# The branch outputs of a hybrid block, parted: pool branch in straight products, delta branch in seven products of halves

## The chip, the cores and the metric

One core of one Trainium2 chip. The metric is the device time of one execution, in microseconds. The engines work side by side, each in order: TensorE (PE) multiplies, VectorE (DVE) and ScalarE (ACT) work on tiles, GpSimd (POOL) and SyncE (SP) mostly start DMAs.

## The reference, cut to what matters

One layer over 16 meta tokens and 512 tokens of width 2048, all float32:

```python
proj = xn @ w_in                       # splits: pool, delta net, gate_pool, gate_dn
y_pool = pooling_mixer(...) * silu(z_pool)        # width 1024
y_dn = gated_deltanet_branch(...)                 # width 2048
merged = sigmoid(gate_pool) * (y_pool @ w_pool_out) + sigmoid(gate_dn) * (y_dn @ w_dn_out)
h = h + merged @ w_o
out = rmsnorm(h[:, N_META:], final_norm_w)
```

The change concerns the line of `merged`: two products, 1024 and 2048 deep, both 2048 wide, over 512 tokens.

## The kernel before, in words

Float32 products at the rate of the short formats: each operand is split into a high part (`xh`, `wh`: a rounded copy, made by ScalarE, line 1198) and a low part (`xl`, `wl`: the difference, made by VectorE, L1753), and each product of tiles is three matmuls: high by high, low by high, high by low. The weight tile (128 x 128) is stationary; the tokens are the moving columns.

**The projection stage** runs 56 blocks of 256 output columns (`NCP`). Most blocks use seven products of halves (the Strassen-Winograd scheme): weights in four quarters, tokens in two halves, contraction in two halves; sums of weight quarters (S1 to S4: `s1`..`s4`, VectorE, L1761 to L1783), sums of x halves made once at the start, seven products numbered 7, 6, 2, 5, 4, 3 and 1 (`NEXT`: product 1 of the following block, issued at the end of the present one), and sums of results (C11, C21, C22). Each product is two chunks of 12 matmuls over 256 tokens (264 where meta tokens count); a ring of five slots (`RINGS`) holds split weights, filled about four chunks ahead (`AHEAD`). The 14 x sets (seven high, seven low) lie in SBUF through the stage (`XPLACE`). The last 16 blocks are the gates: ScalarE puts each through a sigmoid and stores it to `gates_scratch` in DRAM (`gate_tail`, L1583). The two branches' outputs are in DRAM as well (`branch_scratch`, 3072 rows).

**The branch outputs** (`window_b`) replace the x sets by 24 row tiles of `yraw`, split into `yh` and `yl` inside the last gate block and the first windows. Eight pairs of output column tiles `jp`, two tiles `c` each, and three units `u` of 8 row tiles (`u` = 0: pool branch, 1 and 2: delta branch). SP loads each unit's 1 MB of weights, ScalarE and VectorE split it, PE runs 24 matmuls of 512 columns per unit, into bank 0 of `pj[c]` for the pool branch and bank 1 for the delta branch. `merge` on VectorE multiplies both banks with their gates (loaded by POOL's queue, `gate_load`) and adds them into `merged`, which is split into `mh`, `ml` on the way.

**The last product** (`tile_terms`) multiplies `merged` with `w_o`: 4 blocks of 512 columns, 16 row tiles, 4 token tiles, 3 terms; residual, norm and output follow.

Everything on an engine is in the written order; engines meet by semaphores. `pe_chunk` counts chunks, `lo_done` split weights, `peb` finished units.

## Time and profile before

| what | us |
|---|---|
| median of 3 runs | 1894.07 (1891.62 to 1894.8) |
| the profiled execution | 1893.61 |
| its span, first to last instruction | 1891.9 |
| PE busy | 1839.9 (97%) |
| DVE busy | 1294.1 (68%) |
| ACT busy | 996.4 (53%) |
| POOL busy | 120.0 (6%) |

Rows of a profile name a line of the kernel, an engine, an operation and the tiles, output first (`out<-in`). Matmuls are pipelined, so each lasts longer than the distance to the next; a group's mean duration is not what one costs. The granted clock is 1.00 at 2.4 GHz and 0.50 at 1.2 GHz.

### The profile page before, as it was taken

The page shows a single profiled execution, that of the slowest core. Times are in us where ns is not written, and L with a number is a line of the kernel's source. Part 1 is how long each engine was busy: PE and PEld are TensorE (multiplying, and loading weights), DVE is VectorE, ACT ScalarE, POOL GpSimd, SP SyncE. Part 2 cuts the span into 40 slices and gives each one's busy share as a digit, 9 for nine tenths or more (in the row PEclk, how much of TensorE's full clock was granted, in tenths as well). Part 3 has the DMA queues.
Part 4 walks back from the last instruction along what each step waited for, and adds up shares of the span by engine and source line. Part 5 has one row for each costly group of instructions (what it writes and reads, how often), then busy time and mean ns, then how long its engine had stood idle before and what let it go on. Part 6 is the DMA issues. An engine that isn't in the chain of part 4 may idle for free.

```text
span 1891.9 us, 38102 instructions
## 1 busy us (share of the span) xinstructions
PE 1839.9 (97%) x15313; PEld 1727.3 (91%) x15313; DVE 1294.1 (68%) x2404; ACT 996.4 (53%) x2303; POOL 120.0 (6%) x156
## 2 busy tenths in 40 slices
PE   6999999999999999999999999999999999999998
PEld 6999999999899999999999998999998888888886
DVE  7777878777787887878788786777778444344342
ACT  6445456566575756757566675654546222223231
POOL 1100000101010010101001010000000000000000
PEclk9999999999999999999999999999999999999999
DMA  6342465555274555537545454467455434347202
GB/s 190 102 134 64 115 164 149 133 149 155 88 196 137 158 134 145 159 91 197 147 145 136 136 142 133 123 180 201 127 146 165 146 124 142 118 137 289 89 23 89
DMA packets 311000, 264.92 MB, mean 140 GB/s; under 512 B 12201, under 2 KB 266626, under 8 KB 310178
## 3 DMA queue, kind: packets, MB, share of 16 engines
q1 hardware_dynamic: 283712, 197.24, 36.4%
q0 software_dynamic: 12992, 39.57, 7.6%
q10 hardware_dynamic: 14130, 25.81, 3.8%
q8 instruction: 115, 1.88, 0.4%
q14 instruction: 51, 0.42, 0.1%
HBM read 221.03 MB, written 42.60 MB: 139 GB/s over the span
## 4 chain that ended last, share of the span: by engine, by line
PE 76%; DVE 10%; ACT 6%; issue 4%; DMA 3%; POOL 0%; ACTq 0%; DVEq 0%; SPq 0%; POOLq 0%
PE pj L873 35%; PE pj L800 18%; PE pj L832 10%; PE pg L800 10%; PE pt L800 3%; DVE wl L1753 2%; ACT wh L1198 2%; DVE raw L1783 1%; DMA raw<-in_w_in 1%; PE pt L1005 1%; DVE stg L2097 1%; DMA st<-gram_scratch 1%; ACT ktok L1436 1%; ACT L1453 1%; DVE f L1887 0%
## 5 line engine op out<-in xcount | busy, mean ns | idle before, releaser
L873 PE MATMUL pj<-xh,wh 128*128 128x256 f32 (+2 forms) x2568 | 747.7, 291 | 6.7 <-ACT snap L1198 3.0
L873 PE MATMUL pj<-xl,wh 128*128 128x256 f32 (+2 forms) x2568 | 723.5, 282 | 0.0
L873 PE MATMUL pj<-xh,wl 128*128 128x256 f32 (+2 forms) x2568 | 723.4, 282 | 0.0
L1753 DVE TENSOR_TENSOR wl<-raw,wh 128x512 fp32r<-128x512 f32 x742 | 501.0, 688 | 280.7 <-ACT wh L1198 273.1
L1198 ACT ACTIVATE wh<-raw 128x512 fp32r<-128x512 f32 x742 | 452.1, 626 | 401.6 <-PE pj L873 163.9
L873 PEld LDWEIGHTS pj<-xh,wh 128*128 128x128 f32 x2568 | 483.9, 188 | 15.1 <-ACT snap L1198 5.3
L873 PEld LDWEIGHTS pj<-xl,wh 128*128 128x128 f32 x2568 | 484.7, 189 | 0.7 <-issue 0.7
L873 PEld LDWEIGHTS pj<-xh,wl 128*128 128x128 f32 x2568 | 483.5, 188 | 0.0
L832 PE MATMUL pj<-xh,wh 128*128 128x260 f32 (+2 forms) x648 | 186.3, 287 | 3.1 <-DVE wl L1753 3.1
L832 PE MATMUL pj<-xh,wl 128*128 128x260 f32 (+2 forms) x648 | 184.1, 284 | 0.0
L832 PE MATMUL pj<-xl,wh 128*128 128x260 f32 (+2 forms) x648 | 183.8, 284 | 0.0
L1198 ACT ACTIVATE bwh<-rawb 128x256 fp32r<-128x256 f32 x192 | 64.9, 405 | 170.4 <-PE pj L800 169.9
L800 PE MATMUL pj<-yh,bwh 128*128 128x512 f32 x384 | 150.5, 392 | 3.4 <-DVE yl L2301 2.4
L800 PE MATMUL pj<-yl,bwh 128*128 128x512 f32 x384 | 150.0, 391 | 0.0
L800 PE MATMUL pj<-yh,bwl 128*128 128x512 f32 x384 | 149.9, 390 | 0.0
L2296 DVE TENSOR_TENSOR bwl<-rawb,bwh 128x256 fp32r<-128x256 f32 x192 | 69.0, 419 | 85.4 <-ACT bwh L1198 85.4
L832 PEld LDWEIGHTS pj<-xh,wh 128*128 128x128 f32 x648 | 123.2, 190 | 3.6 <-POOL xl L2430 3.4
L832 PEld LDWEIGHTS pj<-xl,wh 128*128 128x128 f32 x648 | 123.4, 191 | 0.2 <-issue 0.2
L832 PEld LDWEIGHTS pj<-xh,wl 128*128 128x128 f32 x648 | 123.0, 190 | 0.0
L2097 DVE SCALAR_TENSOR_TENSOR stg<-xin,convcur,stg 128x528 f32<-128x528 f32 x144 | 109.8, 762 | 8.5 <-ACT stg L1402 7.7
L800 PEld LDWEIGHTS pj<-yh,bwh 128*128 128x128 f32 x384 | 72.5, 189 | 19.3 <-DVE yl L2301 3.3
L800 PEld LDWEIGHTS pj<-yh,bwl 128*128 128x128 f32 x384 | 72.5, 189 | 15.3
(304 smaller groups left out, 2409.3 us busy)
## 6 DMA issues: line engine op xcount, KB each, us to landing
raw<-in_w_in SPq DMA_DIRECT2D x224, 512.0 KB, 4.6
head_scratch<-stg ACTq DMA_DIRECT2D x64, 264.0 KB, 4.1
rawb<-in_w_dn_out SPq DMA_DIRECT2D x16, 1024.0 KB, 6.0
rawb<-in_w_o SPq DMA_DIRECT2D x12, 1024.0 KB, 5.1
kq<-head_scratch SPq DMA_DIRECT2D x8, 1056.0 KB, 9.8
gates_scratch<-stg ACTq DMA_DIRECT2D x32, 256.0 KB, 2.0
rawb<-in_w_pool_out SPq DMA_DIRECT2D x8, 1024.0 KB, 5.3
yraw<-branch_scratch SPq DMA_DIRECT2D x6, 1024.0 KB, 7.7
```

What stands on the lines that cost most here:

```text
L800: return pe.matmul(dst, lhs, rhs, start=start, stop=stop)
L832: mm = pe.matmul(banks[bank][:, c0:TH], w[:, slot, k, :], xx[factor][:, kt, c0:TH], start=chunk in opened and one and k == 0, stop=chunk i ...
L873: mm = pe.matmul(bank[:, c0:TH], w[:, slot, k, :], xx[what][:, kt, c0:TH], start=opens and one and kt == 0, stop=closes and last and kt == ...
L1005: mm = pe.transpose(pt[rows, i * P:(i + 1) * P], src, ident)
L1198: return act.activation(dst, src, ACT.Copy)
L1436: act.activation(ktok[:, at, :], src, ACT.Copy, scale=cur[:, EDEC, at:at + 1]).then_inc(tok_done, 1)
L1453: act.activation(dec[:, 0:XC], dec[:, 0:XC], ACT.Exp, scale=-1.0)
L1753: tt(wl[:, slot, :, :], raw[:, buffer_of(of, par, what), HK * half:HK * (half + 1), :], wh[:, slot, :, :].bitcast(F32), ALU.subtract).then ...
L1783: tt(tile, tile, raw[:, buffer_of(b, par, 2), :, :], ALU.add).then_inc(sum_done, 1)
L2097: dve.scalar_tensor_tensor(acc, xin[:, src_tap:src_tap + T], w, acc, ALU.mult, ALU.add).then_inc(conv_step, 1)
L2296: tt(bwls[u][:, 2 * q:2 * q + 2, :], rawbs[u][:, 2 * q:2 * q + 2, c * P:(c + 1) * P], bwh[:, u, 2 * q:2 * q + 2, :].bitcast(F32), ALU.subt ...
```

## The change

The branch outputs are parted.

*Units.* 16 units of one output column tile each compute `y_pool @ w_pool_out` straight (8 row tiles, 24 matmuls of 512 columns), in turn into the banks `pg[0..2]` and `pt`. VectorE multiplies each with its gate (`unit_weighed`, in place in one of three gate buffers), POOL stores it to `pool_out_scratch` in DRAM, waits for that and loads the gate three units on. Meanwhile VectorE and ScalarE build the seven x sets of the delta branch's output from two buffers `yd`, four steps per unit (`set_steps`, four sums and seven splits for each of four quarters).

*Delta blocks.* `y_dn @ w_dn_out` runs as 8 more blocks of the projection's code (`DN0` to `END`), after a block `PRE` that holds only the first product 1. Their results land in `merged`; VectorE multiplies them with their gates in place (`weighed_by_gate`), and POOL adds the stored pool tiles by an accumulating DMA. The splits of `merged` move: four inside the delta blocks, twelve beside the last product's first block. In the last product the tiles of `w_o` and the splits have other places; the residual rows and the norm's row are loaded ahead of the fifth part of `w_o` and not after the sixth.

The last gate block loses its `yl` parts; eight pool row tiles are split in the gate blocks 10 to 13 (`y_part`), two per block. The loops of `window_b` over column pairs are gone, the new work is written out.

```diff
+ORDER_ALONE = (NEXT,)
...
+PRE = NCP
+DN0 = PRE + 1
+END = DN0 + D // CW
...
+    if b == PRE:
+        return ORDER_ALONE
+    return ORDER_LAST if b in (NCP - 1, END - 1) else ORDER
...
+        NUNIT = D // P
+        SET_SUMS = ((7, "f12", "f22"), (6, "x7", "f11"), (5, "f12", "f11"), (4, "x6", "f21"))
+        SET_SPLITS = (1, 2, 3, 7, 6, 5, 4)
+        STAGE = len(SET_SUMS) + len(SET_SPLITS)
...
+        def unit_buffer(n):
+
+            return 2 if n < 2 else n // 2 % 2
+
+        def unit_ring(n):
+
+
+            return (2, 0)[n % 2]
+
+        def unit_gate(n):
+
+            return (n + 2) % 3
...
+        def m_ready(k):
+
+
+            return mg_done[k // 2 % 2], 32 * (k // 4 + 1)
...
+            def load_unit(jp):
+
+                buffer = unit_buffer(2 * jp)
+                sp.dma_start(unit_raw[buffer], w_pool_out[0, :, jp * CW:(jp + 1) * CW].rearrange("(k p) c -> p k c", p=P)
+                             ).then_inc(w_loaded[buffer], 16)
...
+            sp.wait_ge(lo_done, ALL_SPLITS)
+            load_unit(1)
+            load_unit(2)
+            sp.wait_ge(w_lo, 4)
+            load_stage(0)
             for c in range(2):
                 sp.wait_ge(gate_stored[c], 16 * NGATE)
-            sp.dma_start(yraw[:, 20:24, :], y_rows[:, 20:24, :]).then_inc(yraw_tail, 16)
-            for jp in range(1, D // CW):
-                load_b(jp, False)
+            load_stage(1)
+            sp.wait_ge(w_lo, 8)
+            load_unit(3)
+            sp.wait_ge(x_lo, SET_LO + 3)
+            load_stage(2)
+            sp.wait_ge(w_lo, 12)
+            load_unit(4)
+            sp.wait_ge(x_lo, SET_LO + len(SET_SPLITS) + 3)
+            load_stage(3)
+            for jp in range(5, NUNIT // 2):
+                sp.wait_ge(w_lo, 4 * jp - 4)
+                load_unit(jp)
+            for units, pieces in ((NUNIT - 2, ((RA, 11), (buffer_of(DN0, DN0 % 2, 7), 21))),
+                                  (NUNIT, ((RF, 22), (buffer_of(DN0, DN0 % 2, 2), 12)))):
+                sp.wait_ge(w_lo, 2 * units)
+                for slot, quarter in pieces:
+                    load_raw(slot, quarter, 0, w_dn_out)
+            for b in range(DN0, END - 1):
+                block_loads(b, b % 2, (b + 1 - DN0) * CW, None, w_dn_out)
...
+            pe.wait_ge(y_ready, 2 * PAIRS)
+            pe.wait_ge(x_lo, Y_LO + UK)
+            unit_banks = [pg[0], pg[1], pg[2], pt]
+            for n in range(NUNIT):
+                need(pe, unit_done, n - 3)
+                for half in range(2):
+                    pe.wait_ge(w_lo, 2 * n + half + 1)
+                    for k in range(HK):
+                        kt, ring = HK * half + k, unit_ring(n) + half
+                        for w, yy, one, last in ((wh, yh, True, False), (wh, yl, False, False), (wl, yh, False, True)):
+                            mm = product(unit_banks[n % 4][:, :], w[:, ring, k, :], yy[:, kt, :], one and kt == 0, last and kt == UK - 1)
+                mm.then_inc(w_used, 1)
+
+            for b in range(PRE, END):
+                block_products(b, b % 2, "gate", "gate", no_hook)
...
+                        if b == DN0:
+                            act.wait_ge(unit_stored, 16 * NUNIT - 16)
+                        act.wait_ge(add_done, added(b - 3 if b == DN0 + 1 else b - 2, "C11"))
                         copy(snap[:, par, c0:TH], bank_a[par][:, c0:TH]).then_inc(snap_done, 1)
...
+                        if b == DN0:
+                            act.wait_ge(unit_stored, 16 * NUNIT)
+                        need(act, add_done, added(previous(b), "C22"))
                         copy(snap[:, 3, c0:TH], bank_b[:, c0:TH]).then_inc(snap_done, 1)
...
+            for n in range(NUNIT):
+                if n < NUNIT - 1:
+                    for half in range(2):
+                        unit_split(n + 1, half)
+                else:
+                    for at in range(2):
+                        split_hi(PRE, 0, at)
+                for q, step in set_steps(n):
+                    if step >= len(SET_SUMS):
+                        set_split(q, step - len(SET_SUMS))
+            for at in range(3):
+                split_hi(DN0, DN0 % 2, at)
...
+            def m_split(k):
+
+                act.wait_ge(*m_ready(k))
+                if 4 <= k < 12:
+                    act.wait_ge(pe_chunk, base_of(END))
+                copy(mhs[k], merged[:, k, :]).then_inc(m_hi, 1)
+
+            for b in range(DN0, END):
+                def branch(t, b=b):
+                    j = b - DN0
+                    if t == 0 and j > 0:
+                        last_to_time(b - 1, 1 - b % 2, "gate", merged[:, 2 * j - 2, :])
+                    if t in (4, 6) and j in (4, 5):
+                        m_split(2 * (j - 4) + t // 2 - 2)
+                    if b == END - 1 and t in C_SPLITS:
+                        split_c(0, C_SPLITS.index(t))
+                block_acts(b, b % 2, "gate", "gate", branch, no_hook)
+            last_to_time(END - 1, (END - 1) % 2, "gate", merged[:, KT - 2, :])
...
+            def unit_low(n, half):
+
+                dve.wait_ge(w_hi, 2 * n + half + 1)
+                slot = unit_ring(n) + half
+                own = unit_raw[unit_buffer(n)][:, HK * half:HK * (half + 1), P * (n % 2):P * (n % 2 + 1)]
+                tt(wl[:, slot, :, :], own, wh[:, slot, :, :].bitcast(F32), ALU.subtract).then_inc(w_lo, 1)
+
+            def unit_weighed(n):
+
+                dve.wait_ge(g0_loaded[unit_gate(n)], 16 * (n // 3) + 16)
+                dve.wait_ge(w_used, n + 1)
+                gate = g0[unit_gate(n)]
+                tt(gate, gate, (pg[0], pg[1], pg[2], pt)[n % 4][:, :], ALU.mult).then_inc(unit_done, 1)
+
...
+            gate_block(NCP - 1, 1, into_units, no_hook)
+            dve.wait_ge(pe_chunk, ALL_CHUNKS)
+            for n in range(NUNIT):
+                if n < NUNIT - 1:
+                    for half in range(2):
+                        unit_low(n + 1, half)
+                else:
+                    for at in range(2):
+                        split_lo(PRE, 0, at)
+                if n > 0:
+                    unit_weighed(n - 1)
+                if n == NUNIT - 1:
+                    s3(DN0, DN0 % 2)
+                for q, step in set_steps(n):
+                    set_step(q, step)
+            for at in range(2):
+                split_lo(DN0, DN0 % 2, at)
+            unit_weighed(NUNIT - 1)
+            s2(DN0, DN0 % 2)
+            split_lo(DN0, DN0 % 2, 2)
+
...
+            def weighed_by_gate(j, c):
+
+
+                if c == 1:
+                    dve.wait_ge(g1_loaded[j % 2], 32 * (j // 2) + 32)
+                    dve.wait_ge(add_done, added(DN0 + j, "second"))
+                else:
+                    dve.wait_ge(add_done, added(DN0 + j, "C11"))
+                    dve.wait_ge(last_done, finished(DN0 + j) + 1)
+                tile = merged[:, 2 * j + c, :]
+                tt(tile, tile, g1[:, j % 2, c, :], ALU.mult).then_inc(mg_step, 1)
 
...
+            def gate_load(n):
+
+                pool.dma_start(g0[unit_gate(n)], gates_d[n * P:(n + 1) * P, :]).then_inc(g0_loaded[unit_gate(n)], 16)
+
+            def second_gates(j):
+
+                for c in range(2):
+                    pool.dma_start(g1[:, j % 2, c, :], gates_d[D + j * CW + c * P:D + j * CW + (c + 1) * P, :]).then_inc(g1_loaded[j % 2], 16)
+
+            pool.wait_ge(pe_chunk, ALL_CHUNKS)
+            pool.wait_ge(add_done, counted(NCP, "add"))
             for c in range(2):
-                gate_load(0, c, True)
-            with pool.Fori(1, D // CW) as jp:
-                for c in range(2):
-                    gate_load(jp, c, False)
-
-
+                pool.wait_ge(gate_stored[c], 16 * NGATE)
+            for n in range(3):
+                gate_load(n)
+            for n in range(NUNIT):
+                pool.wait_ge(unit_done, n + 1)
+                pool.dma_start(pool_d[n * P:(n + 1) * P, :], g0[unit_gate(n)]).then_inc(unit_stored, 16)
+                pool.wait_ge(unit_stored, 16 * n + 16)
+                if n + 3 < NUNIT:
+                    gate_load(n + 3)
+            pool.wait_ge(x_lo, SET_LO + 3 * len(SET_SPLITS))
+            for j in range(2):
+                second_gates(j)
+            for j in range(D // CW):
+                for step, c in enumerate((1, 0)):
+                    pool.wait_ge(mg_step, 2 * j + step + 1)
+                    if step == 0 and j > 1:
+                        pool.wait_ge(mg_done[j % 2], 32 * (j // 2))
+                    rows = slice(j * CW + c * P, j * CW + (c + 1) * P)
+                    pool.dma_start(merged[:, 2 * j + c, :], pool_d[rows, :], accum_op=ALU.add).then_inc(mg_done[j % 2], 16)
+                if j + 2 < D // CW:
+                    second_gates(j + 2)
```

## Rows read from the trace of the kernel before

**Rows 1.** The page: busy time by engine, and the chain that ended last.

```profile
PE 1839.9 (97%) x15313; PEld 1727.3 (91%) x15313; DVE 1294.1 (68%) x2404; ACT 996.4 (53%) x2303; POOL 120.0 (6%) x156
...
PE 76%; DVE 10%; ACT 6%; issue 4%; DMA 3%; POOL 0%; ACTq 0%; DVEq 0%; SPq 0%; POOLq 0%
```

**Rows 2.** Stretches: length, busy us (instructions) by engine, granted clock, DMA share, GB/s.

```profile
1203.10:1405.50 202.40, 202.40 (x1713) 202.40 (x1712) 152.50 (x216) 104.85 (x204) 0.72 (x1) 1.00 0.57 159
...
1422.00:1442.20 20.20, 20.20 (x174) 20.20 (x172) 18.96 (x32) 16.98 (x37) 0.00 (x0) 1.00 0.40 131
1442.20:1459.60 17.40, 14.07 (x62) 11.00 (x60) 11.01 (x24) 9.02 (x20) 2.19 (x4) 1.00 0.62 208
1459.60:1465.00 5.40, 5.35 (x16) 4.01 (x16) 4.64 (x11) 3.47 (x11) 0.00 (x0) 0.68 0.36 110
...
1476.00:1709.30 233.30, 233.30 (x1031) 193.19 (x1030) 96.66 (x224) 64.10 (x181) 14.01 (x26) 1.00 0.39 124
1709.30:1752.80 43.50, 43.50 (x193) 36.02 (x193) 19.83 (x31) 15.93 (x28) 0.00 (x0) 1.00 0.84 314
1709.30:1883.40 174.10, 174.08 (x768) 143.80 (x767) 63.20 (x103) 52.15 (x99) 0.00 (x0) 1.00 0.34 127
```

**Rows 3.** The chain of waits in order of time, from 1190 us: start, length, what.

```profile
1203.11 202.35 PE pj L873 x1710
...
1752.82 43.52 PE pj L800 x192
```

**Rows 4.** Timeline of TensorE, 1447 to 1463 us: start, length, what, idle before.

```profile
1448.77 0.47 PE L800 MATMUL pj<-yh,bwh 128*128 128x512 f32 x1 [0.94 <-issue]
...
1456.82 0.39 PE L800 MATMUL pj<-yh,bwl 128*128 128x512 f32 x1
1459.65 0.50 PE L800 MATMUL pj<-yh,bwh 128*128 128x512 f32 x1 [2.44 <-DVE yl L2301]
...
1461.61 0.63 PE L800 MATMUL pj<-yh,bwl 128*128 128x512 f32 x1
```

**Rows 5.** The same chain of waits, 1447 to 1459 us.

```profile
1447.92 0.34 DVE stg L1804
...
1449.00 3.59 DMA gates_scratch<-stg
...
1452.61 5.61 DMA yraw<-branch_scratch
```

**Rows 6.** DMA issues of the whole span: count, KB each, median us to landing.

```profile
gates_scratch<-stg ACTq DMA_DIRECT2D x32, 256.0 KB, 2.0
...
dec<-gate_sum_scratch POOLq DMA_DIRECT2D x8, 512.0 KB, 5.2
```

**Rows 7.** The same from 1400 us to the end.

```profile
gates_scratch<-stg ACTq DMA_DIRECT2D x6, 256.0 KB, 3.9
```

**Rows 8.** DMAs of the tile `gst1a` (a gate, POOL queue), whole span.

```profile
DMA to landing us min/median/max: 2.9/2.9/5.9
```

**Rows 9.** Timeline of POOL: blocks stored to DRAM and the next issue, then a gate.

```profile
1111.54 0.95 POOL L2466 DMA_DIRECT2D gram_scratch<-mk  x1 [16.13 <-DVE mk L2131]
...
1118.82 1.06 POOL L2470 DMA_DIRECT2D st<-gram_scratch  x1 [5.81 <-DMA gram_scratch<-mk]
...
1453.15 0.58 POOL L2514 DMA_DIRECT2D gst0a<-gates_scratch  x1 [244.56 <-DMA gates_scratch<-stg]
```

**Rows 10.** Waits of POOL: us in total, times, longest.

```profile
POOL st L2470 <- DMA gram_scratch<-mk: 30.0, 8, 5.8
```

**Rows 11.** Groups of VectorE, then ScalarE, 1203 to 1442 us: busy, mean ns, idle before.

```profile
L1753 DVE TENSOR_TENSOR wl<-raw,wh 128x512 fp32r<-128x512 f32 x166 | 110.8, 689 | 52.9 <-ACT wh L1198 50.7
L1769 DVE TENSOR_TENSOR raw<-raw 128x1024 f32<-128x1024 f32 x12 | 14.7, 1225 | 1.6
...
L1198 ACT ACTIVATE wh<-raw 128x512 fp32r<-128x512 f32 x165 | 99.7, 627 | 103.8 <-PE pj L873 40.3 <-DMA raw<-in_w_in 27.9 <-DVE raw L1761 20.3
```

More of the change, by code:

```diff
@@ L134, in counted, with loaded, previous, finished @@
         return sum(10 if eight(i) else chunks(i) for i in done)
-    return sum({"sum": (4, 0), "add": (3, 3), "snap": (3, 2)}[what][eight(i)] for i in done)
+    return sum({"sum": (4, 0), "add": (3, 3), "snap": (3, 2)}[what][eight(i)] for i in done if i != PRE)
+def loaded(b):
+    return 16 * b + 16 * (b < PRE)
+def previous(b):
+    return b - 2 if b == DN0 else b - 1
+def finished(b):
+    return b - (b > PRE)
 def base_of(b):
@@ L432, in build @@
-        cwl += [cwl3[:, k, :] for k in range(UK)]
+        yraw = lay.tensor("yraw", [UK, SEQ])
+        yh = lay.tensor("yh", [UK, SEQ], F32R)
+        uraw = lay.tensor("uraw", [UK, CW])
+        lay.skip_to(RING_AT + RINGS * HK * P + 4 * HK * P)
+        g0c = lay.tensor("g0c", [SEQ])
+        assert lay.at == SNAP_AT
+        g0a = lay.tensor("g0a", [SEQ])
+        lay.skip_to(SNAP_AT + 2 * TH + 16)
+        g0b = lay.tensor("g0b", [SEQ])
+        lay.close()
+        g0 = [g0c[:, :], g0a[:, :], g0b[:, :]]
@@ L433, in build @@
+        mls = [ml[:, k, :] for k in range(KT)]
         spare = table[:, :, :, :].rearrange("p a k n -> p (a k n)")
@@ new lines, in set_split, with into_units @@
+            def set_split(q, i):
+                what = SET_SPLITS[i]
+                if i == 0:
+                    act.wait_ge(yd_loaded[q % 2], 32 * (q // 2) + 32)
+                if what > 3:
+                    act.wait_ge(x_sum, SET_SUM + len(SET_SUMS) * q + 1 + [made for made, one, two in SET_SUMS].index(what))
+                copy(set_rows(xh[what], q), set_own(what, q)).then_inc(x_hi, 1)
+            def into_units(t):
+                gate_tail(NCP - 2, 0, t)
+                if t == 10:
+                    for half in range(2):
+                        unit_split(0, half)
@@ L1705, in _ @@
-            for j in range(6):
-                window_b(0, j, "first")
-            with act.Fori(1, UK // 2) as jp:
-                for j in range(6):
-                    window_b(jp, j, "low")
-            for j in range(6):
-                window_b(UK // 2, j, "turn")
-            with act.Fori(UK // 2 + 1, D // CW - 1) as jp:
-                for j in range(6):
-                    window_b(jp, j, "high")
-            for j in range(6):
-                window_b(D // CW - 1, j, "last")
@@ L2360, in _ @@
-            for j in range(6):
-                window_b(0, j, "first")
-            with dve.Fori(1, UK // 2) as jp:
-                for j in range(6):
-                    window_b(jp, j, "low")
-            for j in range(6):
-                window_b(UK // 2, j, "turn")
-            with dve.Fori(UK // 2 + 1, D // CW - 1) as jp:
-                for j in range(6):
-                    window_b(jp, j, "high")
-            for j in range(6):
-                window_b(D // CW - 1, j, "last")
@@ L2372, in _, with no_wait, branch @@
-            m_lo_part(KT - 1)
+                tt(ml[:, k, :], merged[:, k, :], mhs[k].bitcast(F32), ALU.subtract).then_inc(m_lo, 1)
+            def no_wait(c):
+                return None
+            for b in range(DN0, END):
+                def branch(t, b=b):
+                    j = b - DN0
+                    if t == 1 and j > 0:
+                        weighed_by_gate(j - 1, 0)
+                    if t == 10:
+                        weighed_by_gate(j, 1)
+                    if t in (4, 6) and j in (4, 5):
+                        m_low(2 * (j - 4) + t // 2 - 2)
+                    if b == END - 1 and t in C_SPLITS:
+                        split_c(0, C_SPLITS.index(t))
+                block_steps(b, b % 2, "gate", [merged[:, 2 * (b - DN0) + c, :] for c in range(2)], no_wait, branch, no_hook)
```

443 lines of the change are left out of this document (174 added, 269 removed).

## The prediction

> **What bounds the kernel now.** I read the busy times first [rows 1]: TensorE is busy 97% of the span, VectorE 68%; the chain that ended last is 76% TensorE. So a change counts by the TensorE time it removes, unless it opens gaps. The stages [rows 2] show where. From 1203.1 to 1405.5 us, gate projections as products of halves, 256 columns each; 1442.2 to 1709.3 the branch outputs, 512 columns each; 1709.3 to 1883.4 the last product; 8.5 us of tail. In the last three TensorE is always busy except at the start of the branch outputs.
>
> Busy time is no price here, because matmuls overlap (one of 512 columns is shown as 389 ns). The price is the distance from start to start. The chain has 1710 matmuls of 256 columns in 202.35 us, 118.3 ns each, and 192 of 512 columns in 43.52 us, 226.7 ns each [rows 3]; the long stretch of the branch outputs agrees (1031 records in 233.3 us, 226.3 ns) [rows 2]. No row suggests a VectorE or DMA limit in either steady stretch.
>
> At the start of the branch outputs there are two gaps [rows 4]: about 1 us ahead of 1448.77 and 2.6 us at 1456.8 (last start 1456.82, next 1459.65, less one distance). The second comes from the last gate tile: its sum on VectorE (L1804) sat behind the `yl` parts until 1447.9, ScalarE squashed it, its store landed at 1452.6, only then was the last part of `yraw` loaded, 5.61 us, split and used [rows 5]. Then the granted clock is 0.68 for 5.4 us, between the full 2.4 and the half 1.2 GHz [rows 2], with matmuls at 0.63 instead of 0.39 us long [rows 4].
>
> **The change, part by part.**
>
> *The products.* Removed: 8 column pairs x 2 x 24 row tiles x 3 terms = 1152 matmuls of 512 columns, in 267.1 us (1442.2 to 1709.3). At 226.6 ns they are 261.0 us; 6.1 us are the gaps (3.6) and the slower clock and edges (2.5). Added: pool branch, 16 units x 8 tiles x 3 = 384 of 512 columns, 384 x 226.6 = 87.0 us; delta branch, 8 blocks of 7 products of halves x 8 tiles x 3 = 168 of 256 columns, the first product of the first block in the lone block `PRE`, in all 1344 x 118.3 = 159.0 us. Sum 246.0 us. The arithmetic alone is 261.0 - 246.0 = 15.0 us; another 6.1 comes if the start is clean. The ideal eighth of the delta branch (768 x 226.6 = 174.0 us) would be 21.8; 15.0 is left since a matmul of 256 columns costs 118.3 ns and not 113.3.
>
> The Trainium skill (TensorE: Matmul & The Clock Gate, "Back-to-back issue gap") gives an isolated distance of columns/2.4 + 2.5 ns, an estimate of 109.2 and 215.8 ns, and says that weight loads also set the distance. By it the arithmetic gain would be an estimated 768 x 215.8 - 1344 x 109.2 = 19.0 us. The trace stands about 9 to 11 ns above it at both sizes, and I use the trace.
>
> *The start.* The last block of the gates now carries no `yl` parts and only two splits of a weight half. VectorE was busy 18.96 of 20.2 us there and TensorE still had no gap [rows 2]; 75% is its usual load (152.5 of 202.4). So L1804 runs at about 1441 instead of 1447.9, the last sigmoid at 1443, its store lands 2.0 to 3.9 us later [rows 6, 7], at most 1447. The gates load on POOL's queue (0.58 us each, 2.9 to 5.9 us to landing [rows 8, 9]), there by 1450 to 1453. TensorE needs the result of unit 0 out of its bank only for unit 4, at 1442.2 + 4 x 5.44 = 1464; but VectorE, in order, waits for that gate ahead of the low half of unit 3, which is needed at 1458.5. It has 4 us. `yh`, `yl` for the 8 pool tiles are made blocks earlier, the delta tiles are no longer needed at once. I take no gap: the 6.1 us are gained. If the cover went, a gap would cost itself plus up to 2.5 us of clock, as before.
>
> *A unit (5.44 us).* ScalarE: two splits and up to four copies of 128x512 at 0.63 us, at most 3.8 us [rows 11]. VectorE: two low halves, one product with the gate and up to four steps for the seven x sets, 7 x 0.69 alone [rows 11], some 0.6 where they overlap: 4.2 to 4.8 us. Both fit. POOL: after each unit a store to DRAM, a wait until it has landed, and the load three units ahead. No row shows just that. Below: the 256 KB store from ScalarE's queue, 2.0 us [rows 6], and 0.58 each for the two issues [rows 9]: 3.2 us. Above: two stores of blocks to DRAM, from the first issue at 1111.54 until POOL went on at 1118.82, 7.3 us, the longest of eight, with a load's issue 7.9 us [rows 9]; the mean wait of the eight is 30.0/8 = 3.75 us [rows 10]. I take 4.3 us, near the mean, since one store of half the size is what waits: under 5.44, so hidden. Traffic is 8.4 + 4.2 + 4.2 + 4.2 + 2.1 = 23 MB in 87 us, 265 GB/s; the rows have 314 GB/s held for 43.5 us, at a share of 0.84, with TensorE at its pace [rows 2]. Each 1 MB has at least one unit of slack. Cost 0.
>
> *The seam to the delta branch.* `PRE` gives TensorE 24 matmuls, 2.8 us, and product 7 another 2.8 us. In these 5.7 us, after the last unit has freed its ring slots, VectorE does two low halves (1.3), the last gating (0.6), the sum S2 (1.22), then ScalarE a copy (0.63) and VectorE the low half (0.69) [rows 11], after a first copy of 0.63: with the handovers 5.3 us. Slack 0.4 us. The two waits for the last stores (`snap` lies on the gates' tiles) stand ahead of the splits on ScalarE: the store of unit 15 is issued at +2.7, lands near +6.5, and split 6 behind it is needed at +11; slack about 3 us. From nothing to 3 us plus clock; I take 0.5, since the handovers are short.
>
> *A delta block.* Same order as a gate block, with two more VectorE products (2 x 0.6 us, from 75% to about 81% of a block of 168 x 118.3 ns = 19.9 us) and without two sigmoids and stores on ScalarE. The stretch 1422 to 1442 had 94% without a gap [rows 2]. DMA: 2.1 MB of weights, 0.5 of gates and 0.5 accumulated per block, 155 GB/s, as in the gate stage (159). The accumulating DMA of a tile has a block or more before ScalarE splits it; the accumulating DMAs of twice the size in the trace take 5.2 us [rows 6]. The last tile's has 38 us before kt 14. Cost 0.
>
> *The last product.* Its first four tiles are split inside the last blocks; ScalarE and VectorE then have two copies and two subtractions per row tile, 1.3 us each against 2.72. The residual rows and the norm row now precede the fifth weight part: 4.2 + 1.0 + 1.0 MB at 314 GB/s are 20 us, needed after 43.5. Cost 0; 174.1 us and the tail of 8.5 stay.
>
> **Sum.** 246.0 + 0.5 - 267.1 = -20.6 us. The profiled execution took 1893.61 us (span 1891.9): 1873.0. The median of the runs shown, 1894.07, is 0.46 above it, so 1873.5 us is my forecast, a span of 1871.3.
>
> **Rivals.**
> 1. *Late seam.* At the first delta block, or at unit 3, TensorE waits 2 to 6 us, and the clock takes up to 2.5 more. For it: a slack of 0.4 us, and the gap and clock now shown in [rows 4]. Against it: four to five ring slots are filled ahead in every block. 1876 to 1882 us.
> 2. *VectorE too full in the delta blocks.* If the two gating products, which wait in order for ScalarE's last copy and for the gates, delay the splits by their own length, 8 x 0.6 = 5 us: 1878. Against it is the 94% stretch.
> 3. *The other side: POOL's round trip.* If store, landing and next load take longer than 5.44 us, each unit adds the excess to the final waits. Some 4 us are free at the end, so the cost is 16 x (cycle - 5.44) - 4; from 7.0 us on the kernel is slower than before. At the 7.9 us of the longest row it is 35 us, so 1908. For it: 265 GB/s beside these stores. Against: mean 3.75 us at similar traffic, and the store is half the size. The Trainium skill (DMA: Bandwidth & Descriptors, "Anatomy of one DMA — SWDGE (gpsimd) path") says that a DMA's fixed time is mostly the write receipt, heaviest for HBM, and gives 2.0 us + bytes/436 GB/s: an estimate of 2.6 us per store, on the side of my 4.3.
> 4. *The gain does not come*, because another wait takes all of it: within 4 us of now, nothing in the rows for it.
>
> **How the numbers follow.** Forecast 72%, its own range 1871.5 to 1876 (no seam cost at all gives 1873.0, rounding of the distances 1 us to either side, 2.5 us for one small gap). Late seam 14%, VectorE 6%, POOL 6% of which half ends above 1894, no gain 2%. The range 1871 to 1882 leaves out about 1 in 8 and holds the seam and VectorE cases. About 0.2% (3.8 us) can be told from no change here: faster 0.94, same 0.02, slower 0.04.
>
> **What would show it.** Right: 384 matmuls of 512 columns in 87 us, then 1344 of 256 in 159 to 160 without a break, granted clock 1.00 from 1203 to the end of the last product, which starts near 1689; L1804's last run near 1441; POOL's store-to-load cycle under 5 us. Wrong: idle time before the first matmuls of L873 in the delta stage, released by `wl` or `snap`; POOL waiting for `pool_out_scratch` more than 5.44 us a unit; a distance other than 118.3 ns in delta blocks.

## The result, and the profile after

The changed kernel takes 1900.06 us, median of 7 runs (1898.77 to 1901.81), against 1894.07 us before (7 runs, 1889.04 to 1898.34): a ratio of 1.0032, 95% interval 1.0017 to 1.0046. It is slower by 6 us where 20.6 us less were forecast, and lies outside the range. The profiled execution took 1899.81 us with a span of 1897.8.

The page after, the same two rows as [rows 1]:

```profile
PE 1831.1 (96%) x15889; PEld 1747.4 (92%) x15889; DVE 1367.8 (72%) x2424; ACT 1029.0 (54%) x2299; POOL 142.8 (8%) x188
...
PE 67%; DVE 12%; DMA 10%; ACT 6%; issue 5%; POOL 1%; ACTq 0%; DVEq 0%; SPq 0%; POOLq 0%
```

TensorE's share of the chain fell from 76 to 67%, and DMA's rose from 3 to 10%: transfers now end waits that nothing hides. The stretches show where (columns as in [rows 2]):

```profile
1422.00:1442.20 20.20, 20.20 (x173) 20.20 (x172) 15.22 (x23) 10.78 (x21) 0.00 (x0) 1.00 0.28 89
1442.20:1465.00 22.80, 22.80 (x105) 18.96 (x104) 11.87 (x19) 7.69 (x15) 4.06 (x8) 1.00 0.79 271
...
1490.00:1530.00 40.00, 40.00 (x179) 33.14 (x178) 23.57 (x38) 14.32 (x26) 7.60 (x15) 1.00 0.63 197
1530.00:1560.00 30.00, 25.70 (x213) 25.15 (x212) 21.20 (x30) 11.17 (x22) 4.11 (x7) 1.00 0.53 149
...
1600.00:1700.00 100.00, 89.32 (x711) 87.78 (x712) 70.87 (x105) 39.89 (x79) 12.32 (x17) 0.97 0.56 131
```

Up to 1530 us TensorE has no gap: the start of the branch outputs, 3.6 us of gaps before, is clean, and the 16 units take 1442.2 to 1529.8, 87.6 us. From there on it waits: 4.3 us before 1560 at the seam, then 10.7 us in the 100 from 1600 on. The chain of waits, in order of time (start, length, what):

```profile
1203.62 239.27 PE pj L987 x2022
1443.69 4.28 DMA gates_scratch<-stg
1448.60 6.73 DMA g0b<-gates_scratch
...
1589.73 9.26 DMA raw<-in_w_dn_out
...
1683.42 9.69 DMA raw<-in_w_dn_out
...
1701.57 14.41 PE pj L987 x120
```

The gates come as foreseen. But once a block a weight load stands on the chain with 8.5 to 9.7 us (seven blocks, the first with 5.89). The chain's rows of one step in successive blocks (VectorE's fourth sum, `raw` L1876: 1564.56, 1587.97, 1611.64, 1634.91, 1658.70, 1681.65) lie 23.4 us apart on average, where 19.9 were forecast. The branch outputs end at 1715.98: 273.8 us against 267.1 before and 246.5 forecast. The last product is unchanged at 174.1.

### The profile page after: what moved, and what is told of

Read it like the earlier page. It is cut to its first block, busy times and chain, and to the rows that moved or that the text cites. A ratio compares the mean times of both kernels' runs of the same rounds, so it can differ in the third digit from the quotient of the medians.

```text
span 1897.8 us, 39170 instructions
## 1 busy us (share of the span) xinstructions
PE 1831.1 (96%) x15889; PEld 1747.4 (92%) x15889; DVE 1367.8 (72%) x2424; ACT 1029.0 (54%) x2299; POOL 142.8 (8%) x188
## 4 chain that ended last, share of the span: by engine, by line
PE 67%; DVE 12%; DMA 10%; ACT 6%; issue 5%; POOL 1%; ACTq 0%; DVEq 0%; SPq 0%; POOLq 0%
PE pj L987 39%; PE pj L946 10%; PE pg L914 10%; PE pj L914 5%; DVE wl L1846 4%; DMA raw<-in_w_dn_out 3%; PE pt L914 3%; ACT wh L1299 2%; DVE raw L1876 2%; DMA pool_out_scratch<-g0b 1%; DMA pool_out_scratch<-g0a 1%; DMA pool_out_scratch<-g0c 1%; PE pt L1119 1%; DVE stg L2190 1%; DVE raw L1854 1%
## 5 line engine op out<-in xcount | busy, mean ns | idle before, releaser
L987 PE MATMUL pj<-xh,wh 128*128 128x256 f32 (+1 forms) x3016 | 877.3, 291 | 25.3 <-DVE wl L1846 21.2
L987 PE MATMUL pj<-xl,wh 128*128 128x256 f32 (+1 forms) x3016 | 851.4, 282 | 0.0
L987 PE MATMUL pj<-xh,wl 128*128 128x256 f32 (+1 forms) x3016 | 851.1, 282 | 0.0
L1299 ACT ACTIVATE wh<-raw 128x512 fp32r<-128x512 f32 x882 | 535.0, 626 | 560.6 <-PE pj L987 181.5
L1846 DVE TENSOR_TENSOR wl<-raw,wh 128x512 fp32r<-128x512 f32 x854 | 573.8, 688 | 335.9 <-ACT wh L1299 320.9
L987 PEld LDWEIGHTS pj<-xh,wh 128*128 128x128 f32 x3016 | 570.5, 189 | 36.6 <-issue 20.8
L987 PEld LDWEIGHTS pj<-xl,wh 128*128 128x128 f32 x3016 | 571.4, 189 | 0.8 <-issue 0.7
L987 PEld LDWEIGHTS pj<-xh,wl 128*128 128x128 f32 x3016 | 570.3, 189 | 0.0
L946 PEld LDWEIGHTS pj<-xh,wh 128*128 128x128 f32 x648 | 123.3, 190 | 3.6 <-POOL xl L2547 3.4
L946 PEld LDWEIGHTS pj<-xl,wh 128*128 128x128 f32 x648 | 123.6, 191 | 0.2 <-issue 0.2
L946 PEld LDWEIGHTS pj<-xh,wl 128*128 128x128 f32 x648 | 123.1, 190 | 0.0
L1299 ACT ACTIVATE snap<-pj 128x256 f32<-128x256 f32 (+2 forms) x182 | 68.9, 378 | 33.6 <-PE pj L987 22.4
L1862 DVE TENSOR_TENSOR raw<-raw 128x1024 f32<-128x1024 f32 x54 | 66.1, 1224 | 6.3 <-DVE wl L1846 0.5
L1868 DVE TENSOR_TENSOR raw<-raw 128x1024 f32<-128x1024 f32 x54 | 65.8, 1218 | 0.0
L1854 DVE TENSOR_TENSOR raw<-raw 128x1024 f32<-128x1024 f32 x54 | 65.8, 1218 | 0.0
L1876 DVE TENSOR_TENSOR raw<-raw 128x1024 f32<-128x1024 f32 x54 | 65.7, 1218 | 0.0
```

Of the source, the lines that this page charges most:

```text
L946: mm = pe.matmul(banks[bank][:, c0:TH], w[:, slot, k, :], xx[factor][:, kt, c0:TH], start=chunk in opened and one and k == 0, stop=chunk i ...
L987: mm = pe.matmul(bank[:, c0:TH], w[:, slot, k, :], xx[what][:, kt, c0:TH], start=opens and one and kt == 0, stop=closes and last and kt == ...
L1299: return act.activation(dst, src, ACT.Copy)
L1846: tt(wl[:, slot, :, :], raw[:, buffer_of(of, par, what), HK * half:HK * (half + 1), :], wh[:, slot, :, :].bitcast(F32), ALU.subtract).then ...
L1854: tt(tile, tile, raw[:, RA, :, :], ALU.add).then_inc(sum_done, 1)
L1862: tt(tile, tile, raw[:, RF, :, :], ALU.add).then_inc(sum_done, 1)
```

## Where the 27 us went

**In each delta block.** These are slices of 2 us around the weight loads of one block, same columns, of the kernel after:

```profile
1588.00:1590.00 2.00, 2.00 (x20) 2.00 (x19) 2.00 (x3) 0.84 (x2) 1.65 (x3) 1.00 0.46 33
1590.00:1592.00 2.00, 2.00 (x19) 2.00 (x18) 1.51 (x3) 1.13 (x2) 0.00 (x0) 1.00 0.79 161
1592.00:1594.00 2.00, 2.00 (x19) 2.00 (x18) 1.11 (x2) 0.14 (x1) 0.00 (x0) 1.00 0.79 219
1594.00:1596.00 2.00, 2.00 (x19) 2.00 (x18) 0.00 (x0) 0.00 (x0) 0.00 (x0) 1.00 1.12 338
1596.00:1598.00 2.00, 2.00 (x19) 2.00 (x18) 0.00 (x0) 0.00 (x0) 0.00 (x0) 1.00 1.10 278
1598.00:1600.00 2.00, 0.55 (x5) 0.35 (x3) 0.26 (x1) 0.92 (x2) 0.00 (x0) 1.00 0.97 256
1600.00:1602.00 2.00, 1.42 (x7) 1.46 (x8) 2.00 (x3) 0.23 (x1) 0.00 (x0) 0.69 0.60 166
1602.00:1604.00 2.00, 2.00 (x12) 2.00 (x11) 1.90 (x5) 1.15 (x2) 0.40 (x1) 0.50 0.00 0
```

and of a gate block of the kernel before:

```profile
1412.00:1414.00 2.00, 2.00 (x19) 2.00 (x18) 1.81 (x3) 0.70 (x3) 0.00 (x0) 1.00 0.41 65
1414.00:1416.00 2.00, 2.00 (x19) 2.00 (x18) 0.69 (x1) 1.20 (x2) 0.00 (x0) 1.00 1.12 323
1416.00:1418.00 2.00, 2.00 (x19) 2.00 (x19) 1.11 (x2) 0.06 (x1) 0.00 (x0) 1.00 1.23 295
1418.00:1420.00 2.00, 2.00 (x19) 2.00 (x19) 0.47 (x1) 1.14 (x2) 0.00 (x0) 1.00 1.18 291
```

The last number is GB/s. A block's four loads, 2.1 MB, do not spread over its 20 us: they are issued together, when VectorE's last sum frees their slots, and run at about 300 GB/s for 7 us. In the gate block TensorE lives on the splits made ahead, and the loads come just in time. In the delta block the slices from 1588 to 1602 add up to 2.9 MB, and the burst is 5 us longer. What the other 0.8 MB are, POOL's timeline says (start, length, line, operation):

```profile
1587.67 0.85 POOL L2653 DMA_DIRECT2D merged<-pool_out_scratch  x1 [6.88 <-DVE merged L2462]
1588.22 1.43 POOL L2630 DMA_DIRECT2D g<-gates_scratch  x2
```

An accumulation and two gate loads, 256 KB each, are issued from 1.5 us ahead of the weight loads on, and SyncE's row shows the weight loads held up, four issues in 8.02 us where one takes 0.37 in the gate stage:

```profile
1589.18 8.02 SPq L755 DMA_DIRECT2D raw<-in_w_dn_out  x4
```

From issue to landing the weight loads of 1560 to 1716 us take

```profile
DMA to landing us min/median/max: 6.9/8.4/10.2
```

against 4.0/5.5/7.2 for the gate blocks of the kernel before (1290 to 1450). TensorE's timeline shows the price:

```profile
1598.27 0.28 PE L987 MATMUL pj<-xh,wl 128*128 128x256 f32 x1
1600.58 0.39 PE L987 MATMUL pj<-xh,wh 128*128 128x256 f32 x1 [2.02 <-DVE wl L1846]
...
1601.19 0.41 PE L987 MATMUL pj<-xh,wh 128*128 128x256 f32 x1
...
1603.75 0.41 PE L987 MATMUL pj<-xh,wh 128*128 128x256 f32 x1
```

The gap is 2.0 us, and then matmuls start 213 ns apart (12 distances in 2.56 us) instead of 118.3, for some 16 of them, with the granted clock at its lower level of 1.2 GHz (0.50 above). That is 16 x 0.095 = 1.5 us more: 3.5 us in this block. The Trainium skill (TensorE: Matmul & The Clock Gate, Part 1, "Wait — 56ns, not 53.3ns?") has the distance at the low clock as exactly columns/1.2 GHz, an estimate of 213.3 ns for 256 columns. By that rule the trace agrees here, which it did not at the high clock.

The clock does not fall in every block. Of the six blocks with such a gap, three (gaps of 2.10, 2.02 and 2.49 us) go on at the lower clock for some 16 matmuls. The other three (1.63, 1.34 and 2.78 us) keep the full clock, and have two more gaps of 0.3 to 0.4 us each; the longest gap of all is among them:

```profile
1694.69 0.36 PE L987 MATMUL pj<-xh,wh 128*128 128x256 f32 x1 [2.78 <-DVE wl L1846]
```

```profile
1695.00:1698.00 3.00, 2.77 (x24) 2.56 (x22) 2.90 (x6) 1.15 (x2) 0.29 (x1) 1.00 0.03 7
```

Either way a block takes 23.0 to 23.8 us, some 3.5 more than forecast.

**At the seam.** POOL's waits from 1456 to 1540 us (total, times, longest):

```profile
POOL g0a L2625 <- DMA pool_out_scratch<-g0a: 22.3, 4, 7.0
POOL g0b L2625 <- DMA pool_out_scratch<-g0b: 20.7, 5, 5.7
POOL g0c L2625 <- DMA pool_out_scratch<-g0c: 15.8, 4, 5.8
```

Together 58.8 us in 13 rounds, 4.5 each; with the two issues of 0.54, and 1456.34 to 1529.20 for 13 stores, a round is 5.60 us. Forecast was 4.3, and a unit lasts 5.44. The queue also starts late: unit 0 is through TensorE at 1447.6 us, but its gate lands at 1455.3 and its store is issued at 1456.34, 8.7 us behind. Rounds of 4.3 us would have made that good (13 x 1.14 = 14.8 us); rounds of 5.60 add 2.1. How long a round is goes with the traffic. These are the times of two neighbouring stores from issue to landing, columns as above:

```profile
1511.50:1517.50 6.00, 6.00 (x28) 4.99 (x27) 3.67 (x6) 1.15 (x2) 0.50 (x1) 1.00 0.82 257
1518.30:1521.60 3.30, 3.30 (x16) 2.74 (x15) 1.84 (x3) 1.15 (x2) 0.53 (x1) 1.00 0.52 159
```

The chain has 14 stores from 1456 on, of 2.53 to 7.31 us; the longest had 328 GB/s in its time. One does not fit (4.25 us at 314 GB/s). A gate load of POOL's own is issued just ahead of every store but the first and shortest, and no run tells its part from that of the other traffic.

So the queue never catches up: the 14th store goes out 10.8 us behind its unit, and VectorE waits for its landing ahead of its splits (its timeline, then TensorE's):

```profile
1532.62 0.69 DVE L1846 TENSOR_TENSOR wl<-raw,wh 128x512 fp32r<-128x512 f32 x1 [6.72 <-DMA pool_out_scratch<-g0c]
```

```profile
1533.37 0.39 PE L987 MATMUL pj<-xh,wh 128*128 128x256 f32 x1 [2.00 <-DVE wl L1846]
...
1536.64 0.36 PE L987 MATMUL pj<-xh,wh 128*128 128x256 f32 x1 [1.58 <-DVE wl L1846]
...
1540.42 0.36 PE L987 MATMUL pj<-xh,wh 128*128 128x256 f32 x1 [0.72 <-DVE wl L1846]
```

**The account.** From 1529.8 to 1716.0 are 186.2 us for work of 159.0: 27.2 too many. Of these 4.3 are gaps at the seam and 14.6 are gaps after 1560 (3.6, 10.7 and 0.3 by the stretches). Of the remaining 8.3 the lower clock in three blocks makes 4.6 (3 x 16 x 0.095). The other 3.7 stand at the edges of the 15 gaps: idle time is counted from the end of a matmul shown as 0.28 us long, though the next could have started 0.118 after its start (15 x 0.16 = 2.4), and the first matmul after most gaps takes some 0.19 us.

The experiments put four theories against each other. A: POOL's gate loads and accumulations collide with the bunched weight loads. B: `w_dn_out` is slower to read than `w_in` (rows of 8,192 bytes apart instead of 57,472, pieces of 512 bytes in both). C: VectorE is too full (rival 2). D: POOL's round trip makes the seam late (rival 3).

## The experiments

Each time is the median of the runs; "before" on the same chips took 1893.3 to 1894.0 us. The changed kernel itself (1900.06) was not run again beside them, so differences to it lean on "before" having moved by less than 1 us. The edits are shown without the `.then_inc(...)` at the ends of DMA lines; "..." marks lines left out.

One thing helps to read the differences. In the traces TensorE's unbroken run ahead of this stage begins at anything from 1200.6 to 1209.0 us among the changed kernel and its variants, though their instructions up to there are the same. So whole times scatter by some us for reasons ahead of the change. The stretch from the start of that run to the start of the last product leaves this out: 506.2 us in the kernel before, 512.4 in the changed one (one execution each).

**e1_tiny_pool.** The gates of the delta branch from the third block on and all accumulations are cut to 8 numbers in one row; the waits and instructions stay, but the multiplied gates and the added pool branch are missing from the output.

```diff
-pool.dma_start(g1[:, j % 2, c, :], gates_d[D + j * CW + c * P:D + j * CW + (c + 1) * P, :])
+p, n = (P, SEQ) if j < 2 else (1, 8)
+pool.dma_start(g1[0:p, j % 2, c, 0:n], gates_d[D + j * CW + c * P:D + j * CW + c * P + p, 0:n])
-pool.dma_start(merged[:, 2 * j + c, :], pool_d[rows, :], accum_op=ALU.add)
+pool.dma_start(merged[0:1, 2 * j + c, 0:8], pool_d[rows.start:rows.start + 1, 0:8], accum_op=ALU.add)
```

> Leaves out nearly all of the pool queue's traffic in the delta blocks: the gates of blocks 2 to 7 and all sixteen accumulating DMAs move 8 elements of one partition each, so the pool branch and most second gates are missing from the result; every wait and every issue stays. In the changed kernel a delta block takes about 23.4 us where 19.9 were forecast, because the weights of product 1 land 8.5 to 9.7 us after their issue. Theory A (POOL's gate loads and accumulations share the DMA engines with the four weight loads that are bunched into the same 10 us): blocks fall to 19.9 to 20.3 us, the weight loads land in about 5.5 us, whole kernel 22 to 26 us faster than the changed one, about 1875. Theory B (512-byte pieces of rows 8 KB apart are slower to read than those of w_in, rows 57 KB apart): blocks stay at 23 us and the kernel at 1899. Theory C (the two extra products on VectorE shift the loads): blocks stay near 23.

1879.58 us (1878.44 to 1881.81, 3 runs), ratio to before 0.9913 [0.9873, 0.9952]; weight loads land in 5.6 us. 20.5 us come back by taking bytes away, with every instruction of ScalarE and VectorE in place. This bears out A, and speaks against B and C. The 4.6 us above the 1875 expected are the seam, which this edit leaves.

**e2_w_in_layout.** The delta blocks read their weights out of `w_in`, the gate columns, in place of `w_dn_out` (so the products are of other weights).

```diff
-load_raw(slot, quarter, 0, w_dn_out)
+load_raw(slot, quarter, COL_GATE, w_in)
-block_loads(b, b % 2, (b + 1 - DN0) * CW, None, w_dn_out)
+block_loads(b, b % 2, COL_GATE + (b + 1 - DN0) * CW, None, w_in)
```

> The delta blocks read their weights from columns of w_in (the gates') instead of w_dn_out, so the result of the delta branch is another; pieces, sizes and waits are the same, only the distance between rows is 57,472 and not 8,192 bytes. Theory A (POOL's traffic): blocks stay at 23.4 us, loads at 8.4 us, kernel near 1900. Theory B (layout): loads land in about 5.5 us, blocks 19.9 us, kernel about 1875. Theory C: stays.

1900.35 us (1896.19 to 1903.78, 8 runs), ratio 1.0034 [1.0020, 1.0048]; landing 8.3 us. As slow as the changed kernel: B falls.

**e3_gates_from_dn.** The converse in the kernel before: from the fifth on, the gate blocks read `w_dn_out` (other weights again).

```diff
+w = w_in if col < COL_GATE + 4 * CW else w_dn_out
+col = col if col < COL_GATE + 4 * CW else (col - COL_GATE) % D
```

> The kernel before, with the weights of the last 12 of its 16 gate blocks read from w_dn_out (rows 8 KB apart) instead of w_in; the gates' values are others. There is no POOL traffic in that stage. Theory A: gate blocks keep their 19.9 us and the kernel its 1894. Theory B: the loads go from 5.4 to some 8 us and each of the 12 blocks loses about 3.5 us, kernel about 1930.

1895.38 us (1892.85 to 1897.31, 8 runs), ratio 1.0005 [0.9987, 1.0024]. B falls from this side too.

**e4_late_pool.** All work is kept; in six blocks POOL waits, ahead of the second accumulation and so of the gate loads behind it, until the four weight loads have landed.

```diff
+if step == 1 and j + 2 < D // CW:
+    for slot in range(4):
+        pool.wait_ge(raw_loaded[slot], loaded(DN0 + j + 2))
```

> The changed kernel, where POOL's second accumulation and the gate loads of a delta block are held back until the four weight loads of that block have landed. Nothing is left out. Theory A: the weight loads land in about 5.5 us, blocks 19.9 to 20.3 us, kernel about 1876. Theory B and C: blocks stay near 23, kernel 1899. In between (part of each): weight loads 6.5 to 7.5 us, 21 to 22 us a block, 1885 to 1890.

1880.35 us (1879.31 to 1882.60, 3 runs), ratio 0.9936 [0.9913, 0.9958]. The same bytes in another order give back 19.7 us, and the weight loads land in 5.5 us. In its 2-us slices the burst is that of the gate block of before; POOL's timeline shows the issues behind it; and its chain from 1528 us has one row for the rest of the branch:

```profile
1592.00:1594.00 2.00, 2.00 (x20) 2.00 (x19) 1.47 (x4) 0.63 (x1) 0.00 (x0) 1.00 1.01 289
1594.00:1596.00 2.00, 2.00 (x20) 2.00 (x18) 0.33 (x1) 0.00 (x0) 0.00 (x0) 1.00 1.18 302
1596.00:1598.00 2.00, 2.00 (x19) 2.00 (x18) 0.95 (x2) 1.15 (x2) 0.00 (x0) 1.00 1.21 290
```

```profile
1600.41 0.85 POOL L2656 DMA_DIRECT2D merged<-pool_out_scratch  x1 [16.33 <-DMA raw<-in_w_dn_out]
```

```profile
1527.02 6.37 DMA pool_out_scratch<-g0b
...
1534.20 3.18 DMA pool_out_scratch<-g0c
...
1541.49 157.39 PE pj L987 x1320
```

1320 matmuls in 157.39 us, 119.2 ns each, with all of VectorE's work in the blocks: C falls. The two stores above the row are the seam, still waited for, and why this kernel is 4 us above the 1876 expected.

**e5_pipe.** The round trip is shortened: a store is waited for only when the next one has been issued, on two semaphores (`act` and `dve` wait on both).

```diff
-pool.dma_start(pool_d[n * P:(n + 1) * P, :], g0[unit_gate(n)]).then_inc(unit_stored, 16)
-pool.wait_ge(unit_stored, 16 * n + 16)
-if n + 3 < NUNIT:
-    gate_load(n + 3)
+pool.dma_start(pool_d[n * P:(n + 1) * P, :], g0[unit_gate(n)]).then_inc(unit_stored[n % 2], 16)
+if n > 0:
+    pool.wait_ge(unit_stored[(n - 1) % 2], 16 * ((n - 1) // 2) + 16)
+    if n + 2 < NUNIT:
+        gate_load(n + 2)
...
```

> The changed kernel with only the unit stage's order on POOL altered: a store is issued before the wait for the store before it. Nothing is left out. Theory D: the seam's stall of 4 to 6 us goes, the delta blocks stay at 23.4 us each: kernel 1893 to 1896, 4 to 7 us under the changed one. Rival: no difference, 1900.

1894.25 us (1892.27 to 1896.86, 10 runs), ratio 1.0004 [0.9995, 1.0014]: 5.8 us below the changed kernel. That is D's share of its own.

**e6_late_pipe.** e4 and e5 together.

> The changed kernel with two orders on POOL altered and nothing left out: gate loads and the second accumulation of a delta block wait until the block's weight loads have landed (as in e4_late_pool), and in the unit stage POOL issues a store before it waits for the one before it, so that a store's landing no longer stands between two stores. Theory D (what remains after e4 is POOL's round trip of 5.6 to 5.8 us per unit, which makes the first delta block wait for the last stores): the seam's stall of some 8 us goes, TensorE runs from 1203 us to the end of the last product without a gap over 0.5 us, kernel 1872 to 1875. Rival (the two transfers slow each other in the same queue, the round trip stays): kernel stays at 1880.

1876.22 us (1875.72 to 1878.15, 4 runs), ratio 0.9910 [0.9893, 0.9926], 1.2 us above the range expected; 4.1 us below e4, 23.8 below the changed kernel and 17 below the one before. Its stretches are the units, the delta branch and the last product:

```profile
1447.30:1534.40 87.10, 87.10 (x387) 72.13 (x386) 57.44 (x92) 33.75 (x62) 16.70 (x31) 1.00 0.71 238
1534.40:1694.40 160.00, 159.73 (x1345) 159.20 (x1345) 128.85 (x190) 75.83 (x150) 22.68 (x33) 1.00 0.67 171
1694.40:1868.40 174.00, 174.00 (x768) 143.77 (x766) 68.29 (x112) 57.81 (x111) 0.84 (x1) 1.00 0.35 125
```

They are the prediction's 87.0, 159.0 plus 0.5, and 174.1 us, at a full granted clock. On POOL's timeline the stores now wait for VectorE's gating, and no longer for their own landing:

```profile
1510.14 0.54 POOL L2641 DMA_DIRECT2D pool_out_scratch<-g0c  x1 [4.30 <-DVE g0c L2406]
```

The branch outputs are 247.1 us, 20.0 less than before. The whole kernel gains less, 17: this execution began its units 5 us later than the kernel before its branch outputs (1447.3 against 1442.2). That lies within the scatter of the stages ahead named above; from the start of the unbroken run to the last product e6 takes 486.6 us, 19.6 less than before.

**e1_tiny_gates and e1_tiny_add.** Each half of e1's edit alone.

> The changed kernel with the gate loads of delta blocks 2 to 7 cut to 8 elements (those gates are missing from the result); the accumulations stay whole. It splits theory A. If the two gate loads, issued just ahead of the weight loads, do the harm: blocks 19.9 to 20.5 us, kernel about 1880. If the accumulation that is issued with them does it: blocks stay near 23 us, kernel 1898. If both add up: 21 to 22 us, 1887 to 1892.

> The changed kernel with all sixteen accumulating DMAs cut to 8 elements (the pool branch is missing from the result); the gate loads stay whole. The other half of the split: if the gate loads do the harm, blocks stay near 23 us and the kernel near 1897; if the accumulation does, blocks 19.9 to 20.5 us and the kernel about 1880; if both add up, 1887 to 1892.

Tiny gates 1890.88 us (1885.89 to 1895.70, 8 runs), 9.2 below the changed kernel; tiny accumulations 1882.57 (1881.64 to 1883.49, 2 runs), 17.5 below. In each block the two have the same bytes, but just ahead of the weight loads stand two gate loads and only one accumulation; still the gates have about half the accumulations' effect. The two effects together (26.7) are more than that of both edits at once (20.5). Whether that is real is open: the tiny-gates runs spread over 10 us, and in the stretches (one execution each) the effects are 5.4 and 16.3, together 21.7, against 19.9 for both at once.

**e7_plain_add.** The accumulations become plain loads of the same size into the same place (the delta branch is overwritten there).

```diff
-pool.dma_start(merged[:, 2 * j + c, :], pool_d[rows, :], accum_op=ALU.add)
+pool.dma_start(merged[:, 2 * j + c, :], pool_d[rows, :])
```

> The changed kernel with its sixteen accumulating DMAs made plain loads of the same 256 KB into the same tiles (so the delta branch is missing from the result). If an accumulating DMA costs the DMA engines more than its bytes, blocks fall from 23.4 to about 21.5 us and the kernel to about 1887, nearer to the run without accumulations (1882.6). If only the bytes and the moment count: blocks stay at 23.4 us and the kernel at 1900.

1892.72 us (1888.43 to 1896.25, 8 runs), ratio 0.9991 [0.9975, 1.0006]; landing 7.2 us. This is between the two cases expected: 7.3 us of the accumulations' 17.5 hang on their adding; the other 10 hang on bytes and place.

**e8_hold_gates and e9_hold_add.** e4's waits stand ahead of the two gate loads only, or (gate loads first) ahead of the accumulation only.

```diff
 # e8: the second accumulation, then
+for slot in range(4):
+    pool.wait_ge(raw_loaded[slot], loaded(DN0 + j + 2))
 second_gates(j + 2)
 # e9
+second_gates(j + 2)
+for slot in range(4):
+    pool.wait_ge(raw_loaded[slot], loaded(DN0 + j + 2))
 # then the second accumulation
```

> The changed kernel with the gate loads alone held back until the block's weights have landed; the accumulation goes out at once. Nothing is left out. From the cuts (gate loads worth some 9 us, accumulations some 17): about 1890, blocks 22 us.

> The changed kernel with the second accumulation of each block alone held back until the block's weights have landed; the gate loads go out at the same moment as before. Nothing is left out. From the cuts: 1884 to 1888, blocks 21 to 21.5 us, if the accumulation is the dearer part; near 1895 if the gate loads, now alone ahead of the weights, are.

Held gates 1887.99 us (1883.97 to 1892.32, 8 runs), ratio 0.9970 [0.9956, 0.9983]; held accumulation 1885.76 (1883.35 to 1889.90, 8 runs), 0.9952 [0.9936, 0.9969]. Landing 6.7 and 7.0 us. With the accumulation still ahead of the weights (e8) the kernel is 7.6 us above e4, with the gates still ahead (e9) 5.4 us. The ranges of the two overlap, so they do not say which of the two transfers is the dearer.

**e10_before_traffic.** The converse of e4, in the kernel before: in five gate blocks POOL issues one accumulating and two plain DMAs of 256 KB, at the point at which the delta blocks have theirs (the first of the five plain), into tiles that are otherwise free.

```diff
...
+for i, b in enumerate(range(CP_GATE0 + 5, CP_GATE0 + 10)):
+    pool.wait_ge(lo_done, splits(b) + 6)
+    pool.dma_start(yraw[:, 20, :], gates_d[0:P, :], accum_op=ALU.add)   # plain where i == 0
+    for c in range(2):
+        pool.dma_start(yraw[:, 17 + c, :], gates_d[c * P:(c + 1) * P, :])
...
```

> The converse: the kernel before, with three DMAs of 256 KB added on POOL's queue in five of its gate blocks (the 6th to the 10th), at the place where the changed kernel has them in a delta block: after the sixth low half, just ahead of the four weight loads. Two are plain loads, one accumulates (in the first of the five it is plain too); what they load is not used, nothing is left out. Theory A: these blocks grow from 19.9 to about 23.4 us, the weight loads land in 8 us or more, kernel 1893.5 + 4 to 5 x 3.5 = 1907 to 1911. Rival (something else in the delta blocks is needed, such as the fuller VectorE): kernel stays at 1893.5, blocks at 19.9.

1904.83 us (1903.05 to 1905.77, 3 runs), ratio 1.0056 [1.0033, 1.0079]: 10.8 us slower, less than the 13 or more expected (13.3 in the stretch up to the last product, 519.5 against 506.2). Its chain shows waits for weight loads in the disturbed blocks, where the kernel before had one unbroken run of TensorE, and the run is whole again behind them:

```profile
1254.15 9.38 DMA raw<-in_w_in
...
1277.30 9.73 DMA raw<-in_w_in
...
1340.90 96.81 PE pj L876 x816
```

Its weight loads from 1203 to 1340 us, and those of the kernel before in the same time:

```profile
DMA to landing us min/median/max: 4.1/8.0/10.2
DMA to landing us min/median/max: 4.1/5.4/7.2
```

The edit also makes SyncE wait once for the added DMAs before it loads the last `yraw` part of these blocks; no such wait is on the chain.

Extra traffic at this point alone slows gate blocks that have neither `w_dn_out` nor the gating of the delta blocks. A is shown from both sides.

## Why the prediction was wrong

- *The products* were right. e6 has 87.1 and 160.0 us where the sum has 87.0 and 159.5. The trace's distances of 226.6 and 118.3 ns carried over, and an ideal price per column would have forecast a gain that isn't there.
- *The start* was right: L1804's counterpart last runs at 1441.7 (about 1441 said), and TensorE has no gap up to 1530, though the first gate landed at 1455.3, 2 us after the time given. TensorE did not feel that, but POOL's queue did (see the next point).
- *A unit*: "Cost 0" holds for TensorE, but POOL's round trip "4.3 us" is mis-sized: 5.60 us. The mean that it was taken from, 3.75 us [rows 10], is the wait alone. With the two issues ahead of it (0.94 and 0.53 us, medians) those eight stores took 5.2 us until POOL went on; a like reading here is 3.75 + 0.55 + 0.54 = 4.8 us. The rest goes with the traffic: 180 to 202 GB/s beside those eight, up to 328 here. The Trainium skill (DMA: Bandwidth & Descriptors, "Anatomy of one DMA — SWDGE (gpsimd) path") gives an estimate of 2.6 us for such a store. The measurement is above that in every row but the first. Rival 3 named the mechanism, but its term "16 x (cycle - 5.44) - 4" would give nothing for 5.60 (2.6 - 4). It leaves out that the queue starts 8.7 us behind, and the free 4 us were not there: VectorE needs the store of the third unit from the end earlier than the final waits do. e5 measures the whole at 5.8 us.
- *The seam*, 0.5 us, cost 4.3 us of gaps; with the store out of the way (e6) 0.3 us. The handovers were sized rightly, and the store stood in front of them.
- *A delta block* is the step that failed: "DMA: ... 155 GB/s, as in the gate stage (159) ... Cost 0". The measured mean is no higher than that (131 GB/s from 1600 to 1700). It hid that the weights come in a burst of 7 us at 300 GB/s, with no room to land later, and that POOL's three transfers are released by nearly the same event as the four loads, and issued just ahead. The runs show 3.5 us in each of six blocks in its place, 19.7 in all by e4. The prediction looked for the deadline of POOL's transfers (easily kept) and not at whom they delay.
- *VectorE too full* (rival 2) would have cost 5 us; e4 has the blocks at 119.2 ns a matmul with all its work, against 118.3: at most 1.2 us.
- *The last product* was right: 174.1 us. The clock was not full throughout, as a consequence of the gaps.

The rival on the far side got 6 in 100 and the right sign, but not for its own reason: POOL's late stores alone leave a gain of 13 us (e4 has them still). Nothing on the list had two queues meeting.

Still open is whether e1's two halves add up, why the clock fell after three of the gaps and not after the others, and whether the accumulation costs its extra by a second pass over the destination or otherwise; no run tells that apart.

## What to carry to other kernels

Mean bandwidth over a stage does not say whether a transfer is on time: cut the stage into slices of 2 us, look for the burst that the critical queue needs, and ask of every added transfer which event releases it and what is issued within 2 us of it. A transfer with a late deadline belongs behind the burst of one with an early deadline: four waits on POOL in each of six blocks were worth 19.7 us here. A round trip through DRAM on one queue is to be priced at the traffic that will run beside it, and not with a mean from a calmer stage; if it comes near the length of a step, let one store stay in flight (5.8 us).
